# A two-block transformer kernel on one core: norms that work inside the stages around them, and an expert stage that opens with two heads' projections

## What is computed

```python
# first block, on 16 meta tokens + 512 tokens = 528 tokens
for i in range(2):
    hn = rmsnorm(h, norm_w[i])
    y = pool_mixer(hn, ...) if i == 0 else hgrn2_mixer(hn, ...)   # each ends in (2048 -> 1024) @ w_out
    h = h + y
x = rmsnorm(h[:, 16:], final_norm_w)
# second block, on 512 tokens
mod = silu(c) @ w_ada + b_ada            # six vectors: shift1, scale1, gate1, shift2, scale2, gate2
h = rmsnorm(x, norm1_g) * (1 + scale1) + shift1
x = x + gate1 * (attention(h) @ w_o)     # 8 latent-attention heads and 8 forgetting heads
h2 = rmsnorm(x, norm2_g) * (1 + scale2) + shift2
# experts: 8 heads, 16 experts of 16384 each, for every token
qp = h2 @ w_pq; scores = qp . sub_keys; expert, gate = two-stage top 16, softmax
x = x + gate2 * sum(gate * gelu(peer_u[expert] . h2) * peer_v[expert])
```

## Time and profile before

| | |
|---|---|
| median of 3 runs | 3129.91 us (3127.76 to 3131.8) |
| profiled execution | 3130.12 us, of which the span is 3128.3 us |
| granted PE clock, mean | 0.904 |
| busy share of the span | PE 80%, DVE 68%, POOL 37%, ACT 32% |
| HBM | 662.64 MB read; 212 GB/s over the span |
| DMA in 40 slices | low until slice 23, then 8 or 9 tenths to the end |

### The profile page before, as it was taken

The page is one execution under the profiler, slowest core; times in us unless marked ns, Lnnn a source line. Parts: engine busy times, 40 slices in busy tenths (PEclk is TensorE's granted clock), DMA queues, the critical chain, the costliest instruction groups (busy, mean ns, idle before and its releaser), DMA issues. The chain is left out here.

```text
span 3128.3 us, 36172 instructions
## 1 busy us (share of the span) xinstructions
PE 2496.2 (80%) x12276; PEld 1711.4 (55%) x12276; DVE 2133.7 (68%) x3964; ACT 996.2 (32%) x2010; POOL 1166.3 (37%) x952
## 2 busy tenths in 40 slices
PE   6998969999999696687898789866767676766766
PEld 5998969999999694244566434322222222222222
DVE  6357656777778765466334347788878887878876
ACT  2223136666666311232233222222222222222221
POOL 2344346656566230121001033344434344434442
PEclk8999979999999898787999899888888888889888
DMA  3232711221211261000201289999999999999998
GB/s 102 83 97 82 219 50 55 63 59 54 60 54 48 66 204 41 21 8 1 61 21 47 74 310 414 415 427 410 427 427 425 404 427 427 427 397 417 427 427 345
DMA packets 269758, 666.42 MB, mean 213 GB/s; under 512 B 13990, under 2 KB 201547, under 8 KB 203835
## 3 DMA queue, kind: packets, MB, share of 16 engines
q0 software_dynamic: 73728, 536.90, 41.1%
q1 hardware_dynamic: 194906, 127.75, 13.6%
q10 hardware_dynamic: 992, 0.13, 0.0%
HBM read 662.64 MB, written 2.10 MB: 212 GB/s over the span
## 5 line engine op out<-in xcount | busy, mean ns | idle before, releaser
L1900 PE MATMUL peer_py<-peer_uv,peer_diag 128*128 128x512 f32 x1536 | 844.7, 699 | 357.8 <-ACT peer_diag L1830 337.4
L1618 POOL DMA_INDIRECT peer_uv<-k_peer_uv,peer_idx x512 | 505.4, 987 | 778.9 <-PE peer_py L1900 723.4
L1900 PEld LDWEIGHTS peer_py<-peer_uv,peer_diag 128*128 128x128 f32 x1536 | 322.9, 222 | 843.1 <-issue 835.4
L1720 DVE SCALAR_TENSOR_TENSOR peer_spare<-peer_uv,peer_hp 128x1024 bf16<-128x1024 f32 x512 | 622.9, 1217 | 225.3 <-DMA peer_uv<-k_peer_uv,peer_idx 223.5
L1822 ACT ACTIVATE peer_ga<-peer_a 128x2 f32<-128x2 f32 x256 | 52.0, 203 | 825.7 <-DVE peer_spare L1720 825.7
L862 PE MATMUL hgrn_pp<-p2n_hh,hgrn_wh 128*128 128x264 f32 x1024 | 218.7, 295 | 21.1 <-POOL hgrn_wl L733 21.1
L733 POOL TENSOR_TENSOR hgrn_wl<-p2n_w,hgrn_wh 128x1024 fp32r<-128x1024 f32 x64 | 152.5, 2394 | 214.7 <-ACT hgrn_wh L769 214.7
L862 PE MATMUL hgrn_pp<-p2n_hl,hgrn_wh 128*128 128x264 f32 x1024 | 210.1, 287 | 0.0
L862 PE MATMUL hgrn_pp<-p2n_hh,hgrn_wl 128*128 128x264 f32 x1024 | 209.9, 287 | 0.0
L1830 ACT ACTIVATE peer_diag<-keep_ident,peer_wt 128x128 f32<-128x128 f32 x384 | 140.1, 396 | 114.1 <-DVE peer_wt L1727 109.3
L862 PEld LDWEIGHTS hgrn_pp<-p2n_hh,hgrn_wh 128*128 128x128 f32 x1024 | 160.6, 191 | 22.4 <-POOL hgrn_wl L733 21.9
(11 more groups left out here) (371 smaller groups left out, 4854.0 us busy)
## 6 DMA issues: line engine op xcount, KB each, us to landing
p2n_w<-in_hgrn_w_in SPq DMA_DIRECT2D x64, 512.0 KB, 4.1
p1n_w<-in_pool_w_in SPq DMA_DIRECT2D x32, 512.0 KB
pool_out_aw<-in_w_ada SPq DMA_DIRECT2D x16, 768.0 KB, 4.8
hgrn_out_aw<-in_w_ada SPq DMA_DIRECT2D x16, 768.0 KB, 4.6
pool_out_w<-in_pool_w_out SPq DMA_DIRECT2D x8, 1024.0 KB, 7.2
hgrn_out_w<-in_hgrn_w_out SPq DMA_DIRECT2D x8, 1024.0 KB, 7.1
p_w<-in_w_pq SPq DMA_DIRECT2D x8, 1024.0 KB, 6.4
peer_uv<-k_peer_uv,peer_idx POOLq DMA_INDIRECT x512
```

Source lines behind the costliest of these rows:

```text
L1618: pool.indirect_dma_start(out=uv[:, n % DEPTH].rearrange("p w d -> p (w d)"), out_offset=None, in_=io["k_peer_uv"], in_offset=bass.Indirec ...
L1720: dve.scalar_tensor_tensor(out=spare[:, n % 2, :], in0=uv[:, n % DEPTH, 0, :], scalar=1.0, in1=hp[:, t % 2, :], op0=ALU.mult, op1=ALU.mult ...
L1900: last = pe.matmul(py[:, h * 512:(h + 1) * 512], diag[:, products(n) % DIAGS, :], uv[:, n % DEPTH, 1, h * 512:(h + 1) * 512], start=n % (P ...
```

## The change

1. `norm_phase` stays for `norm0` alone. The sums of squares of the other norms are made in the product stage before: after each step ACT squares the finished row and DVE adds it to a running total (for hgrn_out a second total is weighted by the final norm's gain). 
2. A class `Norm` does the rest (two or so matmuls with ones, root, reciprocal, scale, shift or split) inside the block of `hgrn_phase` and of `peer_phase`. `NormPair` does the final norm and the norm behind it together in `latent_phase`: the second's sum of squares is the weighted total times the first's squared factor; `xT` is written afterwards on DVE (`residual`). `gains_phase` moves into it. Three stages fewer.
3. The weight loads that were issued at the start of norm stages are now issued at the start of the block that uses them. In `hgrn_phase` ACT does the high parts of the F and Q weights, and then its part of the norm; POOL makes all eight `hl`, where POOL and DVE made four each.
4. `product_phase`: the first weight block of hgrn_out and attn_out is loaded a stage earlier (`early`); PE's first step goes pass by pass (wh·rh, wl·rh, wh·rl); DVE makes the first 5/8 of the `rl` rows (10 of 16, 5 of 8), POOL the last 3/8 between its first `wl` and its second; SP asks for the second weight block before the first `w_ada` block.
5. `peer_phase`: the indices of a unit no longer wait for the sum of the softmax; the reciprocal (`inverse`) is taken before the weights need it. Only heads 0 and 1 and half of head 2 are projected ahead of the products; units work three heads ahead (s+3) where they worked four. In unit 0 `route` does two pieces at a time for k = 9 to 14.

The core of the diff:

```diff
 class Norm:                                        # new; NormPair likewise, with two roots
+    def act(self, act):
+        act.activation(self.warm[:, :], self.keep["eps"][:, 0:1], ACT.Sqrt)
+        act.wait_ge(self.summed, 1)
+        act.activation(self.rs..., self.sums[:, :, 0:self.tokens // 2], ACT.Sqrt, ...).then_inc(self.rooted, 1)
+        for c in range(KC):
+            act.wait_ge(self.scaled, c + 1)
+            if self.shift is not None:
+                act.activation(self.out[:, c, :], self.out[:, c, :], ACT.Identity, bias=self.shift(c))\
+                   .then_inc(self.ready, 1)
+            else:
+                act.activation(self.parts[0][:, c], self.out[:, c, :], ACT.Copy).then_inc(self.ready, 1)
...
+    def pool(self, pool):
+        if self.parts:
+            for c in range(KC):
+                pool.wait_ge(self.ready, c + 1)
+                pool.tensor_tensor(self.parts[1][:, c], self.out[:, c, :], self.parts[0][:, c].bitcast(F32), ALU.subtract)\
+                    .then_inc(self.low, 1)
...
 def product_phase(...)                             # PE, first step
-                for k in range(kc):
-                    if first:
-                        pe.wait_ge(rl_done, k + 1)
-                    for j, (x, y) in enumerate(((wh, rh), (wh, rl), (wl, rh))):
+                if first:
+                    pe.wait_ge(wh_done, 1)
+                    for j, (x, y) in enumerate(((wh, rh), (wl, rh), (wh, rl))):
+                        if j == 1:
+                            pe.wait_ge(wl_done, m + 3)
+                        for k in range(kc):
...
         @blk.gpsimd
+            low(0, 0)
+            for k in range(by_dve, kc):
+                pool.wait_ge(rh_done, k + 1)
+                pool.tensor_tensor(rl[:, k], rhs[:, k, 0:tokens], rh[:, k].bitcast(F32), ALU.subtract)\
+                    .then_inc(rl_done2, 1)
+            low(1, 1)
...
 def peer_phase(...)
-                    dve.wait_ge(ex_done, r + 1)
-                    note(dve.reciprocal(total[:, r:r + 1], total[:, r:r + 1]))
                 else:
                     need()
                     dve.scalar_tensor_tensor(out=idx[:, r, :], ...)
...
+            def inverse(r):
+                dve.wait_ge(ex_done, r + 1)
+                note(dve.reciprocal(total[:, r:r + 1], total[:, r:r + 1]))
...
-                    if k in (2, 6) and s + 4 < PH:
-                        project(s + 4, 0 if k == 2 else 1)
-                    if k == 12 and s + 4 < UNITS:
-                        scores(s + 4)
+                    if s == 0 and k == 1:
+                        project(2, 1)
+                    if s == 0 and k == 4:
+                        scores(2)
+                    if s == 0 and k in (6, 9):
+                        project(3, 0 if k == 6 else 1)
+                    if s and k in (2, 6) and s + 3 < PH:
+                        project(s + 3, 0 if k == 2 else 1)
+                    if k == (12 if s else 13) and s + 3 < UNITS:
+                        scores(s + 3)
```

More of the change, by code:

```diff
@@ L232, in _, with norm_phase @@
             ch.link(dve.tensor_scalar(lb[:, 1, :], lb[:, 0, :], -1.0, 1.0, ALU.mult, ALU.add))
[L235 to L249, removed]
+def norm_phase(nc, name, x, out, gain, tokens, shift=None, ahead=None):
     keep = nc_keep[0]
@@ L361, in _, with weights, factors @@
         def _(sp):
-            def step(m, b, i, first):
+            def weights(m, b):
                 sp.wait_ge(wl_done, m + 1)
[L364 to L372, removed]
+                sp.dma_start(w[b], view[:, :, ds(m * P, P)]).then_inc(w_in[b], 16)
+            def factors(m):
+                a_view = ada[0].rearrange("(k p) n -> p k n", p=P)
+                for h in range(2):
+                    sp.wait_ge(aw_used, m * 2 + (h + 1))
+                    sp.dma_start(aw[:, h], a_view[:, h * ak:(h + 1) * ak,
+                                                  ds((m + ada[1] * turns) * ADA_COLS, ADA_COLS)])\
+                      .then_inc(aw_in[h], 16)
+            if not early:
+                weights(0, 0)
+            weights(1, 1)
+            if ada:
+                factors(0)
+            with sp.Fori(0, turns // 2 - 1) as i:
+                for b in range(2):
+                    weights(i * 2 + (2 + b), b)
+                    if ada:
+                        factors(i * 2 + (1 + b))
+            if ada:
+                factors(turns - 1)
         @blk.tensor
@@ L419, in _, with low @@
             pool.sem_inc(wl_done, 2)
-            def step(m, b, i, first):
+            def low(m, b):
                 pool.wait_ge(wh_done, m + 1)
-                pool.tensor_tensor(wl[:, b], w[:, b], wh[:, b].bitcast(F32), ALU.subtract).then_inc(wl_done, 1)
-            walk(pool, step)
+                pool.tensor_tensor(wl[:, b], w[b], wh[:, b].bitcast(F32), ALU.subtract).then_inc(wl_done, 1)
+            low(0, 0)
[4 more added lines that the diff above has]
+            low(1, 1)
+            with pool.Fori(0, turns // 2 - 1) as i:
+                for b in range(2):
+                    low(i * 2 + (2 + b), b)
         @blk.vector
@@ L464, in step @@
                     add(m - 1, 1 - b)
+                if not first:
+                    add_squares(m - 1)
+            for gain, total in totals:
+                dve.memset(total[:, :], 0.0).then_inc(sq_added, 1)
             step(0, 0, 0, True)
@@ L843, in _ @@
             high(0, Q)
+            norm.act(act)
             walk(act, step)
@@ L859, in project @@
                 for c in range(begin, end):
+                    if isinstance(n, int) and n == 0 and part == F:
+                        pe.wait_ge(norm.low, c + 1)
                     for j, (x, y) in enumerate(((wh, hh), (wh, hl), (wl, hh))):
@@ L1185, in _ @@
             L, F = la["left"], la["right"]
+            norm.dve(dve)
+            norm.residual(dve)
             ch.link(dve.memset(ones_row[:, :], 1.0))
@@ L1583, in _ @@
         def _(sp):
+            for n in range(2):
+                load(sp, n, n)
             sp.dma_start(count[:, :], io["k_key"][:, 0:TOPK]).then_inc(k_in, 16)
@@ L1877, in _ @@
             turn_h(0)
-            for n in range(1, 4):
-                project(n, 0)
-                project(n, 1)
-                scores(n)
             for c in range(KC):
@@ L2070, in load @@
                 sp.dma_start(w[:, b], view[:, :, n * 2 * P:(n + 1) * 2 * P]).then_inc(w_in[b], 16)
-            def peer_ahead(sp):
-                for b in range(2):
-                    load(sp, b, b)
-            norm_phase(nc, "mod2", xT, h2, col("norm2_g_2"), SEQ,
-                       lambda c: mod[:, 3 * KC + c:3 * KC + c + 1], ahead=peer_ahead)
-            show("hm2", h2[:, :, :])
             peer_phase(nc, io, keep, h2, out, w, w_in, load)
```

315 lines of the change are left out of this document (231 added, 84 removed).

## The result

| | before | changed |
|---|---|---|
| median, us | 3128.84 (3126.55 to 3131.8, 4 runs) | 3083.39 (3082.05 to 3086.45, 4 runs) |
| ratio | | 0.9856 (95%: 0.9839 to 0.9873) |
| profiled execution, us | 3130.12, span 3128.3 | 3083.38, span 3081.6 |

The kernel became 45 us faster (1.4%); 3082 was forecast. That a sum meets the result says little about its terms, so each was read from the two traces. The first view is the windows, in the columns of the earlier trace rows: a stretch of the steady part of the experts in the changed kernel, then a longer one, 800 us, first of the kernel before and then of the changed one.

What follows compares the result with a forecast made beforehand. The prediction took the experts to be bound by gather DMA at 427 GB/s, and everything before the first gather by a chain of stages. Its terms summed to -48.3 us, 3130.1 - 48.3 = 3082, range 3072 to 3094 (3068 to 3100 with rivals).

Steps and rivals of the forecast that it cites:

- (a): pool_out's first steps: PE's second step starts later, waiting for POOL's second wl; +6 us, bounds 0 to +7.
- (c): hgrn_out's first steps: weights already there, but POOL's second wl comes late; +1 us, bounds -5 to +2.
- (e): attn_out's first steps: ACT no longer waits 4.33 for the first weights; -3 us, bounds -1 to -4.
- (b): norm1 inside the hgrn stage: F is done sooner; -8 us, bounds -5 to -9.
- (d): The pair of norms ahead of the latent matmuls, made one chain: -17.5 us, bounds -15 to -19.
- (f): mod2 inside the expert stage: first projection sooner after attn_out's last row; -8.5 us, bounds -6 to -9.5.
- (g): First gather of the experts: index no longer waits for the softmax's sum; -9.9 us, bounds -8 to -9.9.
- (h): DMA time lost at the experts' start: gather 8 follows gather 0 sooner; -8.4 us, bounds -14 to -3.
- Rival 4: Expert part swallows an earlier start: (g) and (h) give nothing, the last product decides; -30 us, 3100, chance 0.02.
- Rival 3: Experts' look-ahead of three heads too short: units' routes wait; at 3 us a unit 3175; chance 0.03.
- windows under 420 GB/s: Sign in the steady expert windows that the forecast is wrong and Rival 3 holds; 427 GB/s was expected.
- Gather 0 some 22 us nearer to attn_out's last row: Sign at the experts' start, told for (g): first gather comes that much sooner, without DVE waiting for ACT.

Runs made afterwards that it cites:

- root_first: The changed kernel with ACT taking the norm's root ahead of the weights' two high parts in the hgrn stage: 3080.33 us, ratio 0.9838 to the kernel before.
- sum_first: The changed kernel with the indices waiting again for the softmax's sum and its reciprocal: 3083.33 us, ratio 0.9848 to the kernel before.
- four_heads_first: The changed kernel with the expert stage's earlier order, four heads projected and scored ahead of the products: 3110.34 us, ratio 0.9934 to the kernel before.
- uv_aligned: The changed kernel with 448 unused bytes a partition ahead of peer_uv, so it begins at a multiple of 512: 3067.05 us, ratio 0.9799 to the kernel before.
- uv_shifted_before: The kernel before with 64 unused bytes a partition ahead of peer_uv: 3144.91 us, ratio 1.0055 to the unedited kernel before.

## Why the prediction was right, and where it was not

**(a), (c), (e), the starts.** Their sizes were right: +8.1 less the 1.5 carried in, +1.0 and -3.1, for +6, +1 and -3. The mechanism was half right. POOL and DVE do block each other, but it isn't POOL that starves: its rows keep a pace of 1.73, and DVE's ten rows, which I put at 302, end at 314.8. What holds PE's second step is the rest of its first, and that waited for DVE's tenth row. POOL's second `wl`, ready at 314.2, comes in through that row, which it held up for 5.00 us. PE's first step even starts 2.7 us sooner than before (293.6 against 296.4), but it takes 24.4 us where it took 13.6. The row of before from which I took the starving, 8.49 for a `wl`, shows one long POOL operation against many short ones of DVE; short against short they alternate, as the rows of norm1 showed.

**The steps.** Here is the real miss. I worked a step out as (1183.8 - 1086.4)/7 = 13.9 and called it PE's. It is a mean over a step of 19 to 20, one of 14 to 15, and five of 12.4; the excess of 9.4 was a stall of PE for weights, and the change to SP's order, which the list of the change names, removes it. The sum has no term for that. The experiments put 19.5 to 20.2 on it for the two stages. A row of the trace of before showed it (7.25 ahead of the third step) and I did not look there.

**(b), (d), (f), the norms.** Right by steps and sizes: -7.4, -16.7, -8.5. In (b) I said that ACT would be late next, behind its weights; root_first shows it, and that only 3 us hang on it, since POOL is the next. In (d) the first latent matmul starts the forecast 17.5 sooner, and 0.8 of it is lost again in the first eight matmuls (6.7 us against 5.9; 5.8 against 6.2 in the other two profiles, so this is no effect of the change). The 1.7 us given back between the latent stage and attn_out are within what one and the same code differs by.

**(g) and (h), the start of the experts.** Their sum was right: from the first projection to the last gather it is 1340.6 to 1343.9 in three profiles with the order before and an aligned target, and 1320.6 to 1324.3 in three with the new order and an aligned target; at the means -19.6, for a forecast of -18.3. The split was wrong. (g) I called a wait gone and worth its 9.9. The first gather does come 9.7 sooner, but only 4.2 of it is the wait for the sum, and sum_first shows these 4.2 worth nothing: the ring holds eight gathers, which take 19.7 to land, and the ninth hangs on the first product and not on the first gather. Whether the other 5.5 are worth anything by themselves is open. What the experiments show as the gain is the first product, 27 us sooner (75.5 to 48.5) with three projections fewer ahead of it; four_heads_first gives back 26.7. Rival 4 was right in that the first gather doesn't decide, and wrong in that (h) gives nothing. In the first 80 us behind the first gather the DMA loses 23.0 us before and 8.4 now (10.4 in uv_aligned), each against its own steady rate of 427, 421 and 427 GB/s; the prediction had 22.8 and 12.

**The rate.** (h) read +6.8. Of its distance to -8.4, 15.2 is the place of `peer_uv`: in uv_aligned the last gather is 1296.7 behind the first, against 1305.1 before, which is -8.4. That the decimals meet is luck: in the other profiles it is 1302.7 and 1301.8 with the old order, 1293.0 and 1294.4 with the new one. I had looked for what the change does to the order and the waits, and not for what its new tile moves in memory.

**The rivals.** Rival 3, the look-ahead of three heads, did not come: a unit takes 40.07 with it when the target is aligned, as with four. My sign for it, windows under 420 GB/s, can't tell it from the target's place: uv_shifted_before, with four heads, shows 420 in such a window.

**A slip in the signs.** "Gather 0 some 22 us nearer to attn_out's last row" counts (e), which lies ahead of that row. (f) and (g) alone give 18.4, and 18.2 was read (59.1 before, 40.9 now).

Thus 3082 was met by luck: two errors of 18.8 and 15.2 have opposite signs. With `peer_uv` aligned the result is 3067, just under the range.

## What to carry to other kernels

A mean over the steps of a loop is no price of a step: list the starts of all steps, and look at each that is longer than the rest. Where a stage is bound by DMA, a new tile ahead of its buffers is part of the change: look at the buffers' addresses in the built program, before and after. And where a ring of buffers is filled at once and its next fill hangs on the first release, look at what the first release waits for before you pay for an earlier first fill.

## What was not expected of the hardware

- The same indirect DMA of 128 rows of 8192 bytes takes 40.73/16 = 2.546 us with its target 64 bytes behind a multiple of 512, 40.07/16 = 2.504 at one, and 2.500 at 256 behind one, in all fourteen profiles (40.0 to 40.1 a unit in six, 40.7 in eight). Its packets of 8192 bytes take 312 and 309 ns at the median.
- Subtractions of 528 elements on DVE and on POOL took turns: 1.75 us for one of each, where DVE alone does one every 0.62 us. Ten on DVE took 21.27 us beside six of POOL's, sixteen 13.93 without them.
